# Two stage seams: order of ScalarE's last work, and which queue issues six sets of transfers

## The chip, the cores and the metric

The kernel runs on one core of one Trainium2 chip. The metric is the device time of one execution in microseconds; the median over runs is compared. The reference time of the kernel before is 3046.53 us, the median of 3 runs (3046.21 to 3046.75).

## The reference, cut to what matters

One transformer-like layer over 2048 latent tokens of width 1024, with 256 context tokens, in float32:

```python
h_x = (x * (1 + mx1) + mx0) @ w_in                    # input projection, 1824 columns
kv  = kv_side(h_x), same for the context               # rms norms, rotary, low-rank expansion by w_ukv
y   = mixer_out(h_x, kv, ...)                          # 6 + 6 attention heads, short conv, @ w_o
x   = layer_norm(ALPHA * x + mx2 * y) * ln1_g + ln1_b
y   = square(relu((x * (1 + mx4) + mx3) @ w_mlp1)) @ w_mlp2   # 1024 -> 4096 -> 1024
x   = layer_norm(ALPHA * x + mx5 * y) * ln2_g + ln2_b
```

Every large product is made of three products of rounded parts (high x high, high x low, low x high), so each operand is split into a "hi" tile (ScalarE copies it into the rounded type) and a "lo" tile (VectorE subtracts). The MLP's two products use seven block products of block sums in place of eight (a Strassen-like scheme): `NP = 7` positions, in the order `ORDER = (3, 5, 2, 4, 1, 7, 6)`.

## The kernel before, in words

The program is six stages, each one block of code with its own instruction stream for SyncE (SP), ScalarE (ACT), VectorE (DVE), GpSimd (POOL) and TensorE (PE): modulate, project, expand, attend, mix, mlp. A stage's block ends for all engines together; the next stage's instructions come behind it on every engine. The order of instructions inside an engine's stream is written out by hand, and semaphores join the streams. Nearly all transfers are issued by SP, a few by ACT; a transfer is issued when its engine's stream comes to it.

**Project (L260 to L608).** Eighteen token tiles of 128 (2 of context, 16 latent). PE projects a tile in four banks, ACT copies the banks out and squares, DVE and POOL normalise and rotate, PE turns the result, ACT rounds it (`out`, L395 on), DVE makes the low parts, SP stores both to DRAM. At the end (`last`) SP waits until everything on PE is done and the stores of tile 15 have landed, and then issues the first loads of the next stage: `load_ckv` part 0, `load_cq` 0, `load_ckv` part 1, `load_cs` 0, the keys of the first head, its queries (`gq_first`), `load_cq` 1, `load_cs` 1. `load_cs` brings the rotary tables of the expansion (384 KB each), `load_cq` the compressed queries of 512 tokens in two parts (512 KB each).

**Expand (L646 on).** Four blocks of 512 tokens. For each, PE makes the rotary part of the queries (it waits for `cq_in[b]`), three query tiles, three key tiles and six value tiles; DVE multiplies by the tables (waits for `cs_in[b]`). Between these, PE makes score products for the running maxima of the first head (L827), the first of which waits for the keys and `gq_first`. SP stores all results and loads what is next. Attend then begins with the loads of the first head (`load_heads`, issued by SP in block 2).

**Mix (L1680 on).** Sixteen token tiles s = 0 to 15. PE multiplies by w_o (L931), DVE adds the residual and normalises (L1906 to L1923), PE turns the normalised tile (L2000), ACT scales it into the MLP's input (`stream`, L1836, eight activations for a tile). Once a pair of tiles is there, POOL makes its block sums (L1967), ACT rounds each of the seven (`highs`, L1867), DVE makes the low parts (`lows`, L1944). Results go to a ring of three places in `area` and from there to DRAM (`s_uc`, SP, L1788), so `highs` waits until the store of three uses earlier has landed; the last sum of the last pair goes into a spare slot instead. ACT's last work of the stage, after the root of tile 15 (L1872), is in this order: `highs` of pair 6, positions 3 to 6; `stream(14)`; `stream(15)`. SP's last work is: stores of the sums at positions 3 to 6, then `load_slot` for positions 5 and 6, four transfers of 1 MB from DRAM into the slots that the MLP multiplies with.

**Mlp (L2016 on).** Its first product needs 32 turns (sixteen for each half); a turn is seven positions, each 12 matmuls of 512 columns (L2718). Positions 0 to 2 of turn 0 were already made in the mix stage (L1665). So PE begins with position 3: ACT rounds the weights (L2321), DVE makes their low part (L2474), PE multiplies. Position 5 waits for slot 5, position 6 for slot 6 (`slot_ready`). SP begins the stage with two semaphore increments for the weights (L2179) that were loaded in mix; POOL waits for them.

Of the kernel before, what the change touches and what calls it, by code (L numbers as in the profile page):

```python
# [210 lines left out]
def stage_project(nc, g, a):  # L211

    with ExitStack() as ctx:
# [56 lines left out]
        def schedule(eng, split, work, out, last, second_in=None):  # L270

            def step(i, c):
                n = i * 2 + c
                if c < CT + TT - 1 and (c != 1 or second_in is None):
                    split(n + 1, c + 1, i + (c + 1) // 2)
                if c == 0 and second_in == "step":
                    split(2, 2, 1)
                work(n, c, c >= CT)
                if c:
                    out(n - 1, c - 1, c > CT)  # L280
            for c in range(CT + 1):
                step(0, c)
            with eng.Fori(0, (TT - 2) // 2) as i:
                step(i, CT + 1)
                step(i, CT + 2)

            last(CT + TT - 1)
# [25 lines left out]
        @block.sync  # L313
        def _(sp):
            sp.dma_start(g_row[:, :], a["g_heads"]).then_inc(tables_in, 16)
            sp.dma_start(inv_n[:, :], a["inv_n"]).then_inc(tables_in, 16)
            sp.dma_start(cs[:, :, :], a["cs_tok"]).then_inc(tables_in, 16)
            for n in range(CT):
                sp.sem_inc(x_in[n], 16)

            def load(n, c):
                sp.wait_ge(ulo_set, n - 1)
                s = c % 2
                sp.dma_start(xt[s][:, :, :], a["x_t"][bass.ds(n - CT, 1)].rearrange("o p k t -> p (o k) t")).then_inc(x_in[s], 16)

            def store(n, is_x, highs=True):
                sp.wait_ge(hi_out, n + 1)
                sp.wait_ge(lo_out, n + 1)
                sp.wait_ge(v_set, n + 1)
                store_kv(sp, n)  # L330
                if is_x:
                    store_x(sp, n, parts=(0, 1) if highs else (1,), conv=highs)

            def step(i, c):
                n = i * 2 + c
                if c < CT + TT - 2:
                    load(n + 2, c)
                if c:
                    store(n - 1, c > CT, c < CT + TT - 1)
            for c in range(CT + 1):  # L340
                step(0, c)
            with sp.Fori(0, (TT - 4) // 2) as i:
                step(i, CT + 1)
                step(i, CT + 2)
            for c in range(CT + TT - 3, CT + TT):
                if c == CT + TT - 2:
                    sp.wait_ge(ulo_set, CT + TT - 1)
                    for done, (at, w, _, _) in zip(w_up_in, EXPANSION):
                        sp.dma_start(at, w).then_inc(done, 16)
                step(0, c)  # L350
            sp.wait_ge(bank_done, banks_before(CT + TT))
            sp.wait_ge(stored, stores_before(CT + TT - 2))
            load_ckv(sp, g, 0, slice(0, CTX))
            load_cq(sp, g, 0)
            load_ckv(sp, g, 1, slice(CTX, CTX + QB))
            load_cs(sp, g, a, 0)
            load_keys(sp, g, 0, g.first_heads_in, slice(0, EARLY_KEYS))
            for half, part in enumerate((slice(0, DH), slice(DH, P))):
                sp.dma_start(g.gq_first[part, :].bitcast(F32), g.qg[half][0:DH, 0:BLK]).then_inc(g.first_heads_in, 16)
            load_cq(sp, g, 1)  # L360
            load_cs(sp, g, a, 1)
            sp.wait_ge(hi_out, CT + TT)
            sp.wait_ge(lo_out, CT + TT)
            sp.wait_ge(v_set, CT + TT)
            sp.wait_ge(stored, stores_before(CT + TT - 1))

        @block.scalar
        def _(act):
            def split(n, c, pair):
                act.wait_ge(modulated, n + 1)  # L370
                need(act, bank_done, banks_before(n - 1))
                nc.scalar.activation(u_hi[c % 2][:, :, :], xt[c % 2][:, :, :], ACT.Copy).then_inc(uhi_set, 1)

            def copy_bank(n, c, b):
                act.wait_ge(bank_done, banks_before(n) + (b + 1))
                c0, cn = BANKS[b]
                nc.scalar.activation(h[c % 2][:, c0:c0 + cn], main[:, b, 0:cn], ACT.Copy).then_inc(bank_out, 1)

            def work(n, c, is_x, banks=len(BANKS)):
                at, hs = banks_before(n), h[c % 2]  # L380
                banks = banks if is_x else 1
                need(act, turned, n - 1)
                need(act, v_set, n - 1)
                for b in range(banks):
                    copy_bank(n, c, b)
                act.wait_ge(bank_out, at + banks)
                need(act, var_set, n)
                width = NORM if is_x else KVR + HKV * DH
                nc.scalar.activation(sq[:, 0:width], hs[:, O_CKV:O_CKV + width], ACT.Square).then_inc(squared, 1)
                if isinstance(n, int) and n == 0:  # L390
                    split(2, 2, 1)
                act.wait_ge(var_set, n + 1)
                nc.scalar.activation(rstd[:, :], var[:, :], ACT.Sqrt).then_inc(std_set, 1)

            def out(n, c, is_x):  # L395
                act.wait_ge(turned, n + 1)
                need(act, stored, stores_before(n))
                for q in range(3 if is_x else 1):
                    nc.scalar.activation(a_hi[:, q], tr_a[:, q * P:(q + 1) * P], ACT.Copy, scale=g.gcol[:, q:q + 1])
                nb = 4 if is_x else 1  # L400
                nc.scalar.activation(b_hi[:, 0:nb], tr_b[:, 0:nb * P].rearrange("p (c t) -> p c t", t=P), ACT.Copy)
                if is_x:
                    nc.scalar.activation(c_st[:, :], tr_c[:, :].rearrange("p (c t) -> p c t", t=P), ACT.Copy)
                nc.scalar.activation(k_hi[:, :], tr_k[0:ROPE, 0:P], ACT.Copy).then_inc(hi_out, 1)
                nc.scalar.activation(v_st[:, :], h[c % 2][:, O_GV:O_GV + P], ACT.Copy).then_inc(v_set, 1)

            def between():
                for done, (at, _, hi, _) in zip(w_up_in, EXPANSION):
                    act.wait_ge(done, 16)
                    nc.scalar.activation(hi, at, ACT.Copy).then_inc(w_up_hi, 1)  # L410

            def last(n):
                work(n, n, True, NORMED)
                out(n - 1, n - 1, True)
                act.wait_ge(hi_out, n)
                store_x(act, n - 1, parts=(0,))
                for b in range(NORMED, len(BANKS)):
                    copy_bank(n, n, b)
                between()
                out(n, n, True)  # L420
            schedule(act, split, work, out, last, second_in="work")
            act.wait_ge(lo_out, CT + TT)

# [209 lines left out]
def load_cq(eng, g, b):  # L633
    for half, t in enumerate((g.cq_hi, g.cq_lo)):
        eng.dma_start(t[b][:, :, :].bitcast(F32), g.cq[half][:, :, b * QB:(b + 1) * QB].rearrange("c p t -> p c t")).then_inc(g.cq_in[b], 16)


def load_cs(eng, g, a, b):
    eng.dma_start(g.e_cs[b][:, :, :], a["cs_rope"][:, :, b * QB:(b + 1) * QB]).then_inc(g.cs_in[b], 16)
# [980 lines left out]
NP = len(ORDER)  # L1620
SLOTS = 8
DIRECT = 3
# [54 lines left out]
def stage_mix(nc, g, a):  # L1677

    with ExitStack() as ctx:
# [81 lines left out]
        def first_half_stored(eng):  # L1761

            for e in range(RING):
                eng.wait_ge(uc_stored[e], 32 * ring_uses(ring_use(3, NP - 1) + 1, e))

        def load_slot(eng, j):

            for part, t in enumerate((g.slot_hi, g.slot_lo)):
                eng.dma_start(raw(t[slot_of(j)]), g.uc[0, j, part]).then_inc(g.slot_in[slot_of(j)], 16)

        @block.sync
        def _(sp):
            sp.dma_start(ln_cols[:, :], a["ln1_cols"]).then_inc(cols_in, 16)
# [33 lines left out]
            store_row(TT - 2)  # L1807
            store_sums(PAIRS - 1, range(0, BEHIND))
            store_row(TT - 1)
            store_sums(PAIRS - 1, range(BEHIND, NP))  # L1810
            first_half_stored(sp)
            sp.wait_ge(y_done, Y_ALL)
            for j in range(DIRECT + 2, NP):
                load_slot(sp, j)
            sp.wait_ge(cols_in, 16)
            sp.wait_ge(mlp_in, 32)

# [1 line left out]
        def _(act):  # L1819
# [48 lines left out]
            for s in range(TT):  # L1868
# [10 lines left out]
                if s == LEFT_AT:  # L1879
                    for pos in range(EARLY_LEFT):  # L1880
                        left_high(pos)
            highs(PAIRS - 1, range(BEHIND, NP))
            stream(TT - 2)
            stream(TT - 1)

        @block.vector
        def _(dve):
# [130 lines left out]
def stage_mlp(nc, g, a):  # L2018

    g.mix_sems.close()  # L2020
    with ExitStack() as ctx:
# [155 lines left out]
        def _(sp):  # L2177
            for q in range(2):
                sp.sem_inc(w1_in[q], 16)  # L2179

            def tail_stores():
                for pos in range(NP):
# [691 lines left out]
```

## Time and profile before

| | us |
|---|---|
| median of 3 runs | 3046.53 |
| the profiled execution | 3052.03 |
| its span | 3050.2 |
| PE busy | 2932.1 (96%) |
| DVE, ACT, POOL busy | 2270.0, 1327.7, 1380.3 |

The span is the time between the first and the last instruction of the profiled execution. A busy time is the sum of an engine's instructions. The seams between the stages are short: expand begins at 417 us, attend at about 495 us, mlp at 1793 us.

### The profile page before, as it was taken

The page shows a single profiled execution, that of the slowest core. Times are in us where ns is not written, and L with a number is a line of the kernel's source. Part 1 is how long each engine was busy: PE and PEld are TensorE (multiplying, and loading weights), DVE is VectorE, ACT ScalarE, POOL GpSimd, SP SyncE. Part 2 cuts the span into 40 slices and gives each one's busy share as a digit, 9 for nine tenths or more (in the row PEclk, how much of TensorE's full clock was granted, in tenths as well). Part 3 has the DMA queues.
Part 4 walks back from the last instruction along what each step waited for, and adds up shares of the span by engine and source line. Part 5 has one row for each costly group of instructions (what it writes and reads, how often), then busy time and mean ns, then how long its engine had stood idle before and what let it go on. Part 6 is the DMA issues. An engine that isn't in the chain of part 4 may idle for free. (4 is left out here: it accounts for less than half of the span.)

```text
span 3050.2 us, 43167 instructions
## 1 busy us (share of the span) xinstructions
PE 2932.1 (96%) x15760; PEld 2201.1 (72%) x15760; DVE 2270.0 (74%) x3170; ACT 1327.7 (44%) x1911; POOL 1380.3 (45%) x833
## 2 busy tenths in 40 slices
PE   5999978999999999999999989999999999999997
PEld 3889865566666566666658768887888888887886
DVE  4445456788887888788777788776777667887788
ACT  3222233444444444444443456555555543433452
POOL 1233324677767867686732244332333144214420
PEclk7999989999999999999999989999999999999998
DMA  6232379524354332434147885447444687897883
GB/s 262 60 87 78 101 234 325 120 74 81 98 119 95 78 81 63 85 80 85 30 149 254 285 311 205 155 152 292 152 153 153 221 299 287 288 315 278 301 289 131
DMA packets 252013, 526.65 MB, mean 173 GB/s; under 512 B 35568, under 2 KB 110832, under 8 KB 240624
## 3 DMA queue, kind: packets, MB, share of 16 engines
q1 hardware_dynamic: 243504, 493.55, 50.4%
q10 hardware_dynamic: 8320, 30.61, 2.6%
q8 instruction: 115, 1.88, 0.3%
q14 instruction: 74, 0.61, 0.1%
HBM read 363.19 MB, written 160.76 MB: 172 GB/s over the span
## 5 line engine op out<-in xcount | busy, mean ns | idle before, releaser
L1369 DVE TENSOR_REDUCE h_mpart<-a_mx 128x1 f32<-128x512 f32 x920 | 537.7, 632 | 153.4 <-PE a_mx L1474 140.6
L1298 POOL TENSOR_TENSOR a_acc_p<-a_acc_p,a_pf 128x1024 f32<-128x1024 f32 x237 | 572.6, 2416 | 152.1 <-ACT a_pf L1349 121.5
L1349 ACT ACTIVATE a_pf<-o_y 128x1024 f32<-128x1024 f32 x432 | 441.8, 1026 | 380.0 <-PE o_y L1521 372.6
L2662 POOL TENSOR_TENSOR stream<-raw_rows 128x512 f32<-128x512 f32 x158 | 217.3, 1377 | 374.6 <-DVE f_wx L2474 360.7
L2671 POOL TENSOR_TENSOR f_y<-f_y,raw_rows 128x1024 f32<-128x1024 f32 x72 | 196.5, 2730 | 350.1 <-DMA raw_rows<-in_w 350.1
L2726 PE MATMUL o_y<-slots 128*128 128x512 f32 x1176 | 298.1, 391 | 1.8 <-DVE slots L2481 1.8
L2718 PE MATMUL o_y<-slots,f_wx 128*128 128x512 f32 x1140 | 266.5, 392 | 4.8 <-DMA slots<-s_uc 4.8
L2726 PEld LDWEIGHTS o_y<-slots 128*128 128x128 f32 x1176 | 221.6, 189 | 49.4 <-DVE slots L2481 3.1
L2718 PEld LDWEIGHTS o_y<-slots,f_wx 128*128 128x128 f32 x1140 | 215.7, 189 | 50.3 <-DMA slots<-s_uc 5.2
L573 PE MATMUL p_main<-win_hi,u_hi 128*128 128x512 f32 (+2 forms) x528 | 196.8, 373 | 15.2 <-PEq L75 14.4
L573 PE MATMUL p_main<-win_hi,u_lo 128*128 128x512 f32 (+2 forms) x528 | 195.2, 370 | 0.0
L573 PE MATMUL p_main<-win_lo,u_hi 128*128 128x512 f32 (+2 forms) x528 | 195.1, 370 | 0.0
L2481 DVE TENSOR_TENSOR slots<-f_y,slots 128x1024 fp32r<-128x1024 f32 x98 | 140.9, 1438 | 71.6 <-ACT slots L2342 70.9
L1539 PE MATMUL a_o<-a_pf,h_gv 128*64 128x512 f32 x864 | 192.8, 595 | 0.0
L1539 PE MATMUL a_o<-a_pf,a_v 128*64 128x512 f32 x864 | 192.7, 595 | 0.0
L2342 ACT ACTIVATE slots<-f_y 128x1024 fp32r<-128x1024 f32 x98 | 104.0, 1061 | 196.6 <-POOL f_y L2671 189.3
L2479 DVE TENSOR_TENSOR slots<-raw_rows,slots 128x1024 fp32r<-128x1024 f32 x98 | 153.3, 1564 | 36.8 <-ACT slots L2334 36.1
L931 PE MATMUL o_y<-slots,low 128*128 128x512 f32 x768 | 179.8, 393 | 0.7 <-PEq L942 0.7
L931 PEld LDWEIGHTS o_y<-slots,low 128*128 128x128 f32 x768 | 143.7, 189 | 32.1 <-issue 2.7
L1521 PE MATMUL o_y<-h_gq,h_gk_hh 64*128 64x512 f32 x864 | 162.2, 402 | 0.2 <-ACT a_pf L1349 0.2
L2474 DVE TENSOR_TENSOR f_wx<-stream,f_wx 128x512 fp32r<-128x512 f32 x158 | 157.9, 999 | 0.6 <-ACT f_wx L2321 0.2
L2726 PE MATMUL o_early<-slots 128*128 128x512 f32 x588 | 151.7, 394 | 4.3 <-DVE slots L2481 4.3
(343 smaller groups left out, 6136.6 us busy)
## 6 DMA issues: line engine op xcount, KB each, us to landing
s_hx<-o_area SPq DMA_DIRECT2D x224, 256.0 KB, 2.6
raw_rows<-s_hx SPq DMA_DIRECT2D x112, 512.0 KB, 4.4
f_y<-in_w SPq DMA_DIRECT2D x104, 512.0 KB, 5.8
raw_rows<-in_w SPq DMA_DIRECT2D x72, 512.0 KB, 5.9
raw_rows<-in_w SPq DMA_DIRECT2D x32, 1024.0 KB, 4.9
s_uc<-o_area SPq DMA_DIRECT2D x76, 256.0 KB, 5.6
raw_rows<-in_w_ada SPq DMA_DIRECT2D x8, 2048.0 KB, 8.8
low<-s_mix SPq DMA_DIRECT2D x32, 512.0 KB, 5.2
```

What stands on the lines that cost most here:

```text
L573: mm = nc.tensor.matmul(main[:, b, 0:cn], lhs[s][:, k], rhs[:, k, c0:c0 + cn], start=(k == 0 and rhs is w_hi and lhs is u_hi), stop=(k == ...
L931: mm = nc.tensor.matmul(y[:, half, :], x_[s % 2][:, k], w_[k][:, half * 512:(half + 1) * 512], start=(k == 0 and n == 0), stop=(k == KD - ...
L1298: nc.gpsimd.tensor_tensor(acc[:, :], left[:, :], pf[(b * KT + kt) % NPF][:, :], ALU.add).then_inc(added_p, 1)
L1349: nc.scalar.activation(pf[n % NPF][:, :], sc[n % 2][:, :], ACT.Exp, scale=SCALES[0 if is_mla(b) else 1]).then_inc(exped, 1)
L1369: nc.vector.reduce_max(mpart[b % 2][:, s + 4 * half, k:k + 1], bank(("pair", c), half)[:, 0:CHUNKS[k][1]], AX.X).then_inc(mx_read, 1)
L1521: mm = nc.tensor.matmul(sc[n % 2][:, half * QB:(half + 1) * QB], w, y[strip, :], start=(m == 0), stop=(m == len(ops) - 1))
L1539: mm = nc.tensor.matmul(o_ps[half * DH:(half + 1) * DH, :], v[0 if is_mla(b) else 1][:, kt], pf[n % NPF][:, half * QB:(half + 1) * QB], st ...
L2474: nc.vector.tensor_tensor(lo, src, hi, ALU.subtract).then_inc(lo_set, 1)
L2662: nc.gpsimd.tensor_tensor(out, w1_part(n, first), w1_part(n, second), plus(sign)).then_inc(sum_set, 1)
L2671: nc.gpsimd.tensor_tensor(y1[cc % YN], y1[cc % YN], y2[k % Y2N], plus(sign)).then_inc(y_sum, 1)
L2718: mm = nc.tensor.matmul(by_pair(bank_at(m)), w[:, k], x[s][:, :, k * P:(k + 1) * P], start=(k == 0 and j == 0), stop=(k == 3 and j == 2))
L2726: mm = nc.tensor.matmul(bank_at(4 * (pr % 2) + tt), x[s][:, f, tok], y[s][:, 2 + f, :], start=(start and j == 0), stop=(stop and j == 2))
```

## The change

Three moves. (1) In mix, `stream(14)` comes on ACT ahead of the rounding at position 3 of the last pair, and `stream(15)` between the roundings at positions 3 and 4. (2) The store of the last sum (position 6) and the loads of slots 5 and 6 leave SP's stream in mix and come in mlp, behind its two semaphore increments; the waits that stood ahead of these loads in mix go too. (3) At the end of project, `load_cs` 0, `load_cq` 1 and `load_cs` 1 leave SP's stream and are issued by ACT, behind its last `out`.

```diff
@@ stage_project, sync
             load_cq(sp, g, 0)
             load_ckv(sp, g, 1, slice(CTX, CTX + QB))
-            load_cs(sp, g, a, 0)
             load_keys(sp, g, 0, g.first_heads_in, slice(0, EARLY_KEYS))
             for half, part in enumerate((slice(0, DH), slice(DH, P))):
                 sp.dma_start(g.gq_first[part, :].bitcast(F32), g.qg[half][0:DH, 0:BLK]).then_inc(g.first_heads_in, 16)
-            load_cq(sp, g, 1)
-            load_cs(sp, g, a, 1)
@@ stage_project, scalar, last
                 out(n, n, True)
+                act.wait_ge(bank_done, banks_before(n + 1))
+                load_cs(act, g, a, 0)
+                load_cq(act, g, 1)
+                load_cs(act, g, a, 1)
@@ stage_mix
+        def store_last_sum(eng):
+
+            p, pos = LAST_SUM
+            for part, at in enumerate(target(p, pos)):
+                eng.dma_start(by_tile(g.uc[p // 4, pos, part][:, p % 4, :]), raw(at)).then_inc(uc_stored[ring_use(p, pos) % RING], 16)
+        g.store_last_sum = store_last_sum
@@ stage_mix, sync
             store_row(TT - 1)
-            store_sums(PAIRS - 1, range(BEHIND, NP))
-            first_half_stored(sp)
-            sp.wait_ge(y_done, Y_ALL)
-            for j in range(DIRECT + 2, NP):
-                load_slot(sp, j)
+            store_sums(PAIRS - 1, range(BEHIND, NP - 1))
@@ stage_mix, scalar
-            highs(PAIRS - 1, range(BEHIND, NP))
             stream(TT - 2)
+            highs(PAIRS - 1, range(BEHIND, BEHIND + 1))
             stream(TT - 1)
+            highs(PAIRS - 1, range(BEHIND + 1, NP))
@@ stage_mlp, sync
             for q in range(2):
                 sp.sem_inc(w1_in[q], 16)
+            g.store_last_sum(sp)
+            for j in range(DIRECT + 2, NP):
+                uc_load(sp, j)
```

## Rows read from the trace of the kernel before

**Rows 1.** The page: busy time by engine; the span in 40 slices.
```profile
PE 2932.1 (96%) x15760; PEld 2201.1 (72%) x15760; DVE 2270.0 (74%) x3170; ACT 1327.7 (44%) x1911; POOL 1380.3 (45%) x833
PE   5999978999999999999999989999999999999997
```
**Rows 2.** Timeline at mlp's seam: start, us, engine line op [idle before <-releaser].
```profile
1787.23 0.68 DVE L1944 TENSOR_TENSOR slots<-o_rows,slots 128x512 fp32r<-128x512 f32 x1
1779.61 1.90 PE L2000 MATMUL o_y<-ident,o_area 128*128 128x128 f32 x8 [3.22 <-DVE o_area L1918]
1772.61 1.03 PE L2000 MATMUL o_t_x<-ident,o_area 128*128 128x128 f32 x8
1787.44 0.39 PE L1665 MATMUL o_y<-slots,o_left_lo 128*128 128x512 f32 x1
1794.91 5.45 PE L2718 MATMUL o_y<-low,f_wx 128*128 128x512 f32 x12 [7.08 <-DVE f_wx L2474]
1800.17 5.67 PE L2718 MATMUL o_y<-slots,f_wx 128*128 128x512 f32 x24
```
**Rows 3.** Chain of waits at the seam into mlp: start us, us, what.
```profile
1792.86 0.02 SPq L2179
1792.90 0.64 ACT f_wx L2321
1793.63 1.14 DVE f_wx L2474
1794.91 10.93 PE o_y L2718 x36
```
**Rows 4.** Timeline of ACT, end of mix.
```profile
1775.96 0.20 ACT L1872 ACTIVATE o_rstd<-o_var 128x1 f32<-128x1 f32 x1 [8.62 <-DVE o_var L1913]
1779.59 0.63 ACT L1867 ACTIVATE o_area<-o_area 128x512 fp32r<-128x512 f32 x1 [3.43 <-DMA s_uc<-o_area]
1784.81 0.64 ACT L1867 ACTIVATE o_area<-o_area 128x512 fp32r<-128x512 f32 x1 [4.58 <-DMA s_uc<-o_area]
1786.42 0.61 ACT L1867 ACTIVATE slots<-o_rows 128x512 fp32r<-128x512 f32 x1
1786.94 2.88 ACT L1836 ACTIVATE o_area<-o_t_x,o_u_cols 128x128 f32<-128x128 f32 x8
1789.68 2.93 ACT L1836 ACTIVATE o_area<-o_y,o_u_cols 128x128 f32<-128x128 f32 x8
```
**Rows 5.** Timeline of SP at the same seam.
```profile
1782.70 5.45 SPq L1788 DMA_DIRECT2D s_uc<-o_area  x6
1788.19 1.15 SPq L1788 DMA_DIRECT2D s_uc<-slots  x2
1789.52 2.26 SPq L1769 DMA_DIRECT2D slots<-s_uc  x4
```
**Rows 6.** Timeline of SP, end of project.
```profile
411.24 0.72 SPq L639 DMA_DIRECT2D e_cs<-in_cs_rope  x1
...
414.66 0.59 SPq L635 DMA_DIRECT2D e_cq_hi<-s_cq  x1
415.29 0.47 SPq L635 DMA_DIRECT2D e_cq_lo<-s_cq  x1
415.80 0.62 SPq L639 DMA_DIRECT2D e_cs<-in_cs_rope  x1
```
**Rows 7.** Timelines of PE and ACT around the start of expand.
```profile
417.12 0.55 PE L810 MATMUL e_ring<-e_ckv_hi,low 128*128 128x256 f32 x1 [9.51 <-PEq L213]
411.81 0.29 ACT L405 ACTIVATE v_st<-h 128x128 f32<-128x128 f32 x1
426.76 0.50 PE L827 MATMUL e_mx<-h_gk_hh,e_gq_first 128*128 128x512 f32 x1 [2.32 <-DMA e_gq_first<-s_qg]
```
**Rows 8.** Transfer issues at 1789.52 to 1791.78: count, KB, us to landing; first and last.
```profile
slots<-s_uc SPq DMA_DIRECT2D x1, 1024.0 KB, 6.5
slots<-s_uc SPq DMA_DIRECT2D x1, 1024.0 KB, 12.1
```
**Rows 9.** Stretches: us, busy by engine (PE PEld DVE ACT POOL), PEclk, DMA share, GB/s.
```profile
1780.00:1785.00 5.00, 5.00 (x21) 4.26 (x20) 2.64 (x3) 0.42 (x2) 0.00 (x0) 0.69 1.02 413
1794.90:1800.20 5.30, 5.29 (x13) 4.14 (x14) 4.55 (x3) 3.22 (x7) 5.30 (x4) 0.50 0.99 417
```
**Rows 10.** The same view of stretches, expand.
```profile
412.00:440.00 28.00, 18.46 (x66) 14.86 (x67) 13.39 (x25) 6.43 (x13) 4.89 (x3) 0.74 1.03 299
440.00:470.00 30.00, 28.43 (x120) 22.25 (x119) 21.38 (x35) 11.68 (x21) 7.45 (x5) 0.97 1.04 371
470.00:500.00 30.00, 21.49 (x88) 16.70 (x88) 16.99 (x31) 10.49 (x19) 10.45 (x11) 0.88 1.02 329
```
**Rows 11.** Transfers: `gq_first` (last, issued 414.0), `load_cs` 1 (415.80), `gk_ll` (487.81).
```profile
e_gq_first<-s_qg SPq DMA_DIRECT2D x1, 256.0 KB, 12.7
e_cs<-in_cs_rope SPq DMA_DIRECT2D x1, 384.0 KB, 15.5
h_gk_ll<-s_kg SPq DMA_DIRECT2D x1, 576.0 KB, 11.5
```
**Rows 12.** Timeline of PE, start of attend.
```profile
499.37 0.80 PE L1474 MATMUL a_mx<-h_gk_hh,h_gq 64*128 64x512 f32 x2 [0.81 <-DMA h_gk_ll<-s_kg]
```
**Rows 13.** Transfers in mix: ACT's load issued at 1772.8, SP's store at 1772.5.
```profile
low<-s_uc ACTq DMA_DIRECT2D x1, 1024.0 KB, 8.7
s_uc<-o_area SPq DMA_DIRECT2D x1, 256.0 KB, 10.7
```

## The prediction

> **What bounds the kernel now.** I began with the page [rows 1]. PE is busy for 2932.1 of 3050.2 us, and only the first slices and a few later ones are not full. Gaps on PE are therefore the only place where moved work on ACT or SP can pay, and all of them together are 118 us. The change touches two seams, so I next read the chain of waits and the timelines there.
>
> Into mlp: PE makes its last early product at 1787.44 + 0.39 = 1787.83 and its first mlp product at 1794.91, 7.08 us idle [rows 2]. The chain reads back from there: PE waits for DVE's low part, that for ACT's rounding at 1792.90, and this for SP's first instruction of the stage at 1792.86 [rows 3]. The reader is to see which engine was last in mix: ACT, whose second `stream` ends at 1789.68 + 2.93 = 1792.61 [rows 4]. DVE was done at 1787.91 [rows 2], SP at 1789.52 + 2.26 = 1791.78 [rows 5]. So it takes 0.3 us from the last engine's end to the next stage's start (1792.61 to 1792.90), and 2.0 us more until PE works (1792.90 to 1794.91).
>
> Into expand: SP is last. Its final issue ends at 415.80 + 0.62 = 416.42 [rows 6], and PE begins at 417.12 after 9.51 us idle; ACT was done at 412.10 [rows 7]. That is 0.7 us from SP's end to PE's work.
>
> **The change part by part.**
>
> *Streams on ACT.* ACT is idle for 3.43 us until 1779.59 and again for 4.58 us until 1784.81, both times because a store of the ring has not landed [rows 4]. `stream(14)` takes 2.88 us. What it reads has been there since before the root at 1775.96, so it runs from 1776.2 to 1779.1 and position 3 stays at 1779.59. `stream(15)` waits for PE's turning, which ends at 1779.61 + 1.90 = 1781.5 [rows 2]. It takes 2.93 us and ends at 1784.5, 0.3 us ahead of the ring's landing at 1784.81. Positions 4 to 6 stay where they are, the last at 1786.42 + 0.61 = 1787.03. Cost 0, covered by the two waits; without that cover it would be their 5.8 us, as before. ACT's end moves from 1792.61 to 1787.03, 5.6 us earlier.
>
> *Store and slot loads on SP.* SP's last issue in mix is now the store at position 5, which ends at 1782.70 + 5.45 = 1788.15 [rows 5]. DVE (1787.91) and PE (1787.83) end just ahead, so SP is last. The next stage starts at 1788.15 + 0.3 = 1788.45, and PE can begin at 1788.45 + 2.0 = 1790.45, which is 4.45 us earlier than 1794.91.
>
> What is late next: the slots. In mlp SP issues the two stores (1.15 us) and then the four loads (2.26 us), six transfers in all [rows 5]. The first load is issued at about 1788.5 + 1.15 + 0.15 = 1789.8, against 1789.52 before. From first issue to last landing it took before: last issued at 1791.3, landed 12.1 us later, at 1803.4; the first landed at 1789.52 + 6.5 = 1796.0 [rows 8]. The data thus comes no earlier than before: 1803.4 to 1803.7. Before, PE took up slot 6 after the 24 matmuls of positions 4 and 5, at 1800.17 + 5.51 = 1805.7, 2.3 us after the landing. Now position 3 runs from 1790.45 for 5.26 us (it took 1794.91 to 1800.17 [rows 2], at a granted clock of 0.50, the lower level of 1.2 GHz [rows 9]), positions 4 and 5 take 5.5 us, and PE stands ready for slot 6 at 1801.2. It waits 2.4 us, to 1803.6. The gain of the seam is 1805.7 - 1803.6 = 2.1 us, not 4.45. Half of it again may go: PE has a new pause of 2.4 us, and after the pause of 3.22 us at 1779.6 eight small matmuls took 1.90 us, as against 1.03 us for their like at 1772.61 [rows 2], and the granted clock of that stretch is 0.69, part of it at the lower level [rows 9]. I price the lower clock at 0.8 us, between 0 (the pause is short enough) and 1.6 us. Seam: -1.3 us, bounds -4.45 (slots come early) and -0.3.
>
> Behind ACT's first four roundings stands its wait for the last sum's store. This is now issued at 1788.5 rather than 1788.19 and ACT arrives 4.4 us earlier. The stores took some 4 us to land, to 1793.3, and ACT's fourth rounding ends at 1798.2 - 4.4 = 1793.8; cost 0. POOL's first sums only wait for the semaphore increments, which stand ahead of SP's transfers. SP's next weight load and tail stores come behind six issues rather than none, 3.4 us, but they begin 4.4 us sooner; cost 0.
>
> *Tables and queries on ACT's queue.* SP drops four issues: 0.72 + 0.62 us [rows 6] for the tables and about 1.1 us for the two of `load_cq`, with gaps 2.6 us. It ends at 413.9. ACT gets four issues behind 412.10, at 0.5 to 0.6 us each: it ends at 414.4. Expand starts at 415.1 instead of 417.1. This is 2.0 us on PE, and I count none of it as a gain. The stretches show why [rows 10]: the DMA share is 1.03, 1.04 and 1.02 in the three stretches from 412 to 500 us. Every transfer waits in a backlog, 15.5 us for the last table [rows 11]. Attend begins on a transfer too: `gk_ll`, issued at 487.81, lands 11.5 us later at 499.3, and PE's first product of attend starts at 499.37 [rows 11, 12]. The change moves no byte away and starts none before 412, when the DMA engines are already full. What ends the stage is the total of bytes by the rate. So: 0 us. Bounds: below, 2.0 us gained, if attend follows PE; above, 3 us lost, as in the second rival.
>
> The Trainium skill bears on this ("DMA: Bandwidth & Descriptors", section "Queues, rings and completion order"): each DMA engine serves its queues in turn, a packet at a time, so a second queue adds no bandwidth but lets its transfers overtake those of the first. By that rule the loads on ACT's queue would share the engines with `gq_first`, which two of the three stood behind; the sum would then be that of the second rival. This trace has it in mix only, and agrees there: the store below took 10.7 us.
>
> **Sum.** -1.3 + 0 = -1.3 us. Against the profiled execution's 3052.03 us (a span of 3050.2 and 1.8 around it) this is 3050.7; its distance to the median of the runs, 5.5 us, is that of profiling and the same on both sides. From the median: 3046.53 - 1.3 = 3045.2 us. Behind both seams PE's slices are at nine tenths or more [rows 1], so I take it that what is won at a seam stays.
>
> **The rivals.**
>
> *Both seams pay in full.* Landing is set by the time of issue and not by the backlog, and DMA in expand catches up. For it: the first pause of 7.08 us is real and ACT alone ends it. Against it: landings at 1803.4 and 499.3, each within 2.4 us of the need. -4.45 - 2.0 = -6.4 us, 3040.1 us. Chance 0.10. One seam in full and the other as forecast, -3.3 to -4.5 us, 3042 to 3043 us: 0.20.
>
> *The other side: the first score product waits for `gq_first`.* Place: PE at 426.76, where it already waits 2.32 us for this very transfer [rows 7]. Of the bytes on ACT's queue, 384 KB stood ahead of it before; the other 1.4 MB (1024 + 384 KB) stood behind, and landed 4.6 us later (426.7 to 415.80 + 15.5 = 431.3) [rows 11]. If both queues share the engines evenly, `gq_first` lands near 431, up to 4.6 us late, and PE with it. Of this PE can win back what it waited for other things in this block, about 1.9 us; the rest, 2.7 us, counts from the point at which SP's stores come so late that the DMA backlog runs dry. Then +2.7 - 1.3 = +1.4 us, 3047.9 us; with a further pause of PE's clock, up to 3049. For it: in mix a store of 256 KB on SP's queue took 10.7 us to land while ACT's queue had its loads of 1 MB under way [rows 13], against 4 us at the end of the stage, so the two queues do share. Against it: the backlog later in the stage (11.5 us for `gk_ll` [rows 11]) is far longer than 2.7 us. Chance 0.18.
>
> *Nothing comes of it.* The pause for slot 6 costs the whole gain in clock (1.6 us) and landing is 0.3 us later: 0 to -0.3 us, 3046.4 us. Chance 0.15.
>
> The forecast, -0.5 to -2.5 us, has the remaining 0.37.
>
> **How the numbers follow.** The range takes in one seam paid in full together with most of the other (-6) and the second rival with its clock term (+2.5): 3040.5 to 3049.0. Outside is part of the first rival and what no row shows. 0.2% is 6.1 us, about what a measurement of this kernel can tell from no change. Faster by more needs both seams in full: of the 0.10 a little over half, 0.06. Slower by more would need a loss that no row bounds: 0.03. Within 0.2%: 0.91.
>
> **What the changed profile would show.** ACT's last activation of mix near 1787.0, the `stream` groups at 1776.2 and 1781.6 (all times shifted by whatever project brings), and SP as the last engine. PE's gap into mlp falls from 7.1 to about 2.6 us, and a new wait of 2 to 3 us appears before position 6, put down to `slots<-s_uc`. If that wait is missing, I was wrong on the landing and the gain is 4 us. In expand PE starts 2 us earlier, its wait at the first L827 is longer than 2.32 us, and the first product of attend stands within 1 us of 499.4. If it stands at 497.4, DMA was not the bound; if it stands beyond 501, the second rival holds.

## The result: slower by about 7 us, and the profile after

| | before | after |
|---|---|---|
| median of 13 runs each, side by side | 3044.9 | 3052.7 |
| lowest to highest | 3041.1 to 3050.5 | 3045.8 to 3057.6 |
| span of the profiled execution | 3050.2 | 3053.1 |

The ratio is 1.0024, with an interval of 1.0015 to 1.0033: 7.3 us slower, between 4.6 and 10. The forecast was 1.3 us faster. Single runs of one kernel lie up to 10 us apart or more, so the spans of single profiles do not rank kernels here. What a profile can give is the distance between two events of one seam, and I read it that way throughout.

The page of the changed kernel says what [rows 1] said: the same work, and PE busy nearly all the time.

```profile
PE 2932.0 (96%) x15760; PEld 2202.2 (72%) x15760; DVE 2264.5 (74%) x3170; ACT 1328.5 (44%) x1911; POOL 1378.3 (45%) x833
PE   5999978999999999999999979999999999999997
```

**The seam into expand.** First the timeline of SP: its first and last loads at the end of project, then the stores of the late tile and the next loads of expand.

```profile
409.57 0.49 SPq L631 DMA_DIRECT2D e_ckv_hi<-s_ckv  x1
414.21 1.30 SPq L358 DMA_DIRECT2D e_gq_first<-s_qg  x2
...
419.54 2.88 SPq L699 DMA_DIRECT2D s_kn<-e_st_hi  x1
422.46 4.87 SPq L699 DMA_DIRECT2D s_kn<-e_st_lo  x1
437.56 0.35 SPq L631 DMA_DIRECT2D e_ckv_hi<-s_ckv  x1
```

SP ends its project work at 415.5 now (it was 416.42 [rows 6], with the stage 1.3 us later as a whole). Between 427.3 and 437.56 it issues nothing. The view of waits says for what: a store of the queries' low part. Before the change it was the last of SP's own late stores (`s_vg<-v_st`, issued at 424.61, landed 8.6 us later) that let SP go on, at 433.23. Now that store has landed at 434.2 (419.02 + 15.2), and the wait goes on for another 3.3 us. The columns are us in total, times, longest.

```profile
SPq L631 <- DMA s_qg<-b_lo: 10.2, 1, 10.2
```

Who issued that store? ACT did. Its timeline shows the four new transfers, and then the four stores of tile 15 that ACT always had to make at the start of expand (`late_x`, L294 and L295; SP stores the rest).

```profile
411.46 0.70 ACTq L640 DMA_DIRECT2D e_cs<-in_cs_rope  x1
412.19 0.76 ACTq L636 DMA_DIRECT2D e_cq_hi<-s_cq  x1
412.98 0.88 ACTq L636 DMA_DIRECT2D e_cq_lo<-s_cq  x1
413.89 0.60 ACTq L640 DMA_DIRECT2D e_cs<-in_cs_rope  x1
...
418.51 0.45 ACTq L294 DMA_DIRECT2D s_cq<-a_hi  x1
419.00 0.49 ACTq L295 DMA_DIRECT2D s_qg<-b_hi  x1
419.52 5.48 ACTq L294 DMA_DIRECT2D s_cq<-a_lo  x1
425.03 2.32 ACTq L295 DMA_DIRECT2D s_qg<-b_lo  x1
427.39 0.60 ACT L738 ACTIVATE e_st_hi<-e_ring 128x512 fp32r<-128x512 f32 x1 [8.51 <-issue]
```

The reader is to see the second numbers. Issuing a store of 128 KB took 5.48 us and the next one 2.32 us, where the two before them took 0.45 and 0.49. ACT itself stands still for 8.51 us ("issue"). Before the change the same two issues took 0.51 and 0.49 us and the last of them began at 420.89. The view of transfers gives its landing: the last store took 12.5 us, so it landed at 425.03 + 12.5 = 437.5, which is when SP goes on.

```profile
s_qg<-b_lo ACTq DMA_DIRECT2D x1, 192.0 KB, 12.5
```

The stretches of the changed kernel show what this does to the DMA engines (columns as in [rows 9]; [rows 10] has 1.03 for the first).

```profile
412.00:440.00 28.00, 17.93 (x59) 14.28 (x60) 11.28 (x22) 7.50 (x16) 4.86 (x3) 0.71 0.94 257
434.00:436.00 2.00, 2.00 (x7) 1.56 (x7) 1.05 (x2) 0.20 (x1) 0.00 (x0) 0.69 0.99 328
436.00:438.00 2.00, 2.00 (x10) 1.60 (x10) 1.29 (x2) 1.89 (x4) 0.58 (x1) 1.00 0.10 34
438.00:440.00 2.00, 1.78 (x9) 1.31 (x8) 1.91 (x4) 1.63 (x4) 1.80 (x1) 1.00 0.69 169
```

From 436 to 438 us the engines have next to nothing to do (share 0.10, 34 GB/s). The same slices of the kernel before:

```profile
434.00:436.00 2.00, 1.35 (x7) 0.90 (x5) 0.19 (x1) 0.82 (x2) 1.86 (x1) 1.00 0.91 222
436.00:438.00 2.00, 0.75 (x4) 0.66 (x4) 2.00 (x4) 1.14 (x3) 0.00 (x0) 1.00 1.00 396
```

This profile is the mildest of the five with the old project end. In the others (e2, e3, e5 and g1, below) the thinnest slice of 2 us between 432 and 440 us has a share of 0.83, 0.51, 0.32 and 0.37. So the old order thins at this place too. What sets the change apart is how much is lost: from 412 to 440 us the five have shares of 0.98 to 1.03, and the three profiles with this move 0.94, 0.92 and 0.92.

On PE (to be laid beside [rows 7] and [rows 12]): expand begins earlier, the first score product later, and attend later.

```profile
416.21 0.55 PE L811 MATMUL e_ring<-e_ckv_hi,low 128*128 128x256 f32 x1 [6.42 <-PEq L213]
429.74 0.79 PE L828 MATMUL e_mx<-h_gk_hh,e_gq_first 128*128 128x512 f32 x1 [5.63 <-DMA e_gq_first<-s_qg]
...
503.23 0.79 PE L1475 MATMUL a_mx<-h_gk_hh,h_gq 64*128 64x512 f32 x2
```

I count from SP's first load of the seam, to be free of what came before it. PE starts 6.6 us behind it (8.9 before), `gq_first` is there at 20.2 (18.5), attend's first product at 93.7 (91.1). So the move does start PE 2.2 us sooner, and the stage ends 2.5 us later.

Attend's first product waits for no transfer in the changed kernel. The loss comes in earlier, where ACT has to wait for the landing of a store of queries before it rounds the next ones (first line before, second after):

```profile
483.38 1.08 ACT L737 ACTIVATE e_st_hi<-e_ring 128x512 fp32r<-128x512 f32 x2 [6.29 <-DMA s_qn<-e_st_lo]
486.88 1.08 ACT L738 ACTIVATE e_st_hi<-e_ring 128x512 fp32r<-128x512 f32 x2 [7.64 <-DMA s_qn<-e_st_lo]
```

Counted from SP's first load this is 75.1 us before and 77.3 after (77.6 in e1 and 77.3 in e4, which have the same move). Thirteen of the fourteen profiles have this wait, and in all of them attend's first product follows 15.7 to 17.1 us behind it. Most of the 2.5 us is thus there at a transfer's landing. I have not followed wait by wait how the dry slice at 436 us leads to the late landing at 486.

**The seam into mlp.** ACT (beside [rows 4]), SP (beside [rows 5]) and PE (beside [rows 2]), in three fences.

```profile
1779.25 2.89 ACT L1840 ACTIVATE o_area<-o_t_x,o_u_cols 128x128 f32<-128x128 f32 x8
1789.50 0.63 ACT L1871 ACTIVATE o_area<-o_area 128x512 fp32r<-128x512 f32 x1 [7.36 <-DMA s_uc<-o_area]
1790.03 2.89 ACT L1840 ACTIVATE o_area<-o_y,o_u_cols 128x128 f32<-128x128 f32 x8
1792.78 0.66 ACT L1871 ACTIVATE o_area<-o_area 128x512 fp32r<-128x512 f32 x1
...
1793.81 0.66 ACT L1871 ACTIVATE slots<-o_rows 128x512 fp32r<-128x512 f32 x1
```
```profile
1790.95 5.09 SPq L1796 DMA_DIRECT2D s_uc<-o_area  x6
1796.69 0.82 SPq L1776 DMA_DIRECT2D s_uc<-slots  x2
1797.56 2.21 SPq L2124 DMA_DIRECT2D slots<-s_uc  x4
```
```profile
1775.93 1.03 PE L2005 MATMUL o_t_x<-ident,o_area 128*128 128x128 f32 x8
1798.58 5.46 PE L2726 MATMUL o_y<-low,f_wx 128*128 128x512 f32 x12 [11.13 <-DVE f_wx L2482]
1803.84 6.06 PE L2726 MATMUL o_y<-slots,f_wx 128*128 128x512 f32 x24
1811.81 5.74 PE L2726 MATMUL o_t_x<-slots,f_wx 128*128 128x512 f32 x24 [1.91 <-DMA slots<-s_uc]
```

`stream(14)` lies in the first wait, as meant. Then the ring's place for position 3 is free 13.6 us after the turning of tile 14 (1789.50 - 1775.93), against 7.0 us before (1779.59 - 1772.61 [rows 2, 4]). When it comes, the places for the next positions are free too, so `stream(15)` stands in nobody's shadow: position 4 follows directly behind it. PE's pause into mlp is 11.13 us, where 7.08 was to become 2.6. SP is the last engine of the stage, and PE's wait for slot 6 is there, 1.91 us. From the turning of tile 14 to position 6 it is 35.9 us, against 33.1.

### The profile page after: what moved, and what is told of

Read it like the earlier page. It is cut to its first block and busy times, and to the rows that moved or that the text cites. A ratio compares the mean times of both kernels' runs of the same rounds, so it can differ in the third digit from the quotient of the medians.

```text
span 3053.1 us, 43165 instructions
## 1 busy us (share of the span) xinstructions
PE 2932.0 (96%) x15760; PEld 2202.2 (72%) x15760; DVE 2264.5 (74%) x3170; ACT 1328.5 (44%) x1911; POOL 1378.3 (45%) x833
## 5 line engine op out<-in xcount | busy, mean ns | idle before, releaser
L574 PE MATMUL p_main<-win_hi,u_hi 128*128 128x512 f32 (+2 forms) x528 | 197.7, 374 | 15.1 <-PEq L75 14.4
L2489 DVE TENSOR_TENSOR slots<-f_y,slots 128x1024 fp32r<-128x1024 f32 x98 | 148.7, 1518 | 69.8 <-ACT slots L2350 69.0
```

Source lines behind the costliest of these rows:

```text
L574: mm = nc.tensor.matmul(main[:, b, 0:cn], lhs[s][:, k], rhs[:, k, c0:c0 + cn], start=(k == 0 and rhs is w_hi and lhs is u_hi), stop=(k == ...
L2489: nc.vector.tensor_tensor(slot_lo[s][:, 2:4, :], y1[cc % YN], slot_hi[s][:, 2:4, :], ALU.subtract).then_inc(clo, 1)
```

## The experiments

Ratios are to the kernel before, run beside them on the same chip, with their intervals; 0.1% is 3 us. Two distances of each profile are read besides: **A**, from SP's first load of the seam to attend's first product (before 91.1; the five profiles with the old project end have 90.1 to 92.0), and **B**, from the turning of tile 14 to position 6 in mlp (before 33.1).

### The parts alone

*e1_project: only move 3.*

```diff
 # stage_project, sync
-            load_cs(sp, g, a, 0)
-            load_cq(sp, g, 1)
-            load_cs(sp, g, a, 1)
 # stage_project, scalar, last
                 out(n, n, True)
+                act.wait_ge(bank_done, banks_before(n + 1))
+                load_cs(act, g, a, 0)
+                load_cq(act, g, 1)
+                load_cs(act, g, a, 1)
```

> Only the third move: the tables and load_cq 1 on ACT's queue at the end of project, all else as before. From SP's first load of the seam (s_ckv to e_ckv, 408.24 us before, 409.57 after the whole change) to PE's first product of attend it took 91.1 us before and 93.7 us with the whole change. Theory (the queues share, gq_first comes late): 93 to 95 us here too, PE's wait at the first L827 near 5.6 us instead of 2.3 us, and the run 2 to 5 us slower than before. Rival (the loss is in mix): 91 to 92 us and a run within 1.5 us of before.

Measured: 1.0017 (1.0008 to 1.0027), 5.2 us slower. A is 94.0. ACT's issues stall as in the whole change, and the DMA engines run dry at the same point:

```profile
417.88 6.43 ACTq L294 DMA_DIRECT2D s_cq<-a_lo  x1
424.34 2.73 ACTq L295 DMA_DIRECT2D s_qg<-b_lo  x1
427.12 0.60 ACT L738 ACTIVATE e_st_hi<-e_ring 128x512 fp32r<-128x512 f32 x1 [9.82 <-issue]
```
```profile
434.00:436.00 2.00, 2.00 (x8) 1.45 (x7) 1.29 (x2) 0.43 (x2) 0.00 (x0) 0.81 0.28 92
436.00:438.00 2.00, 2.00 (x10) 1.60 (x10) 1.32 (x3) 2.00 (x4) 0.47 (x1) 1.00 0.31 41
```

This one move is slower by itself.

*e2_mix: moves 1 and 2, project as before.*

```diff
 # stage_mix, sync
-            store_sums(PAIRS - 1, range(BEHIND, NP))
-            first_half_stored(sp)
-            sp.wait_ge(y_done, Y_ALL)
-            for j in range(DIRECT + 2, NP):
-                load_slot(sp, j)
+            store_sums(PAIRS - 1, range(BEHIND, NP - 1))
 # stage_mix, scalar
-            highs(PAIRS - 1, range(BEHIND, NP))
             stream(TT - 2)
+            highs(PAIRS - 1, range(BEHIND, BEHIND + 1))
             stream(TT - 1)
+            highs(PAIRS - 1, range(BEHIND + 1, NP))
 # stage_mlp, sync, behind the two increments
+            g.store_last_sum(sp)
+            for j in range(DIRECT + 2, NP):
+                uc_load(sp, j)
```

> Only the first two moves: stream(14) and stream(15) between the roundings, last store and slot loads in mlp; project as before. In the profile of the whole change the ring store that ACT waits for at position 3 landed 15.3 us after its issue, against 8.9 before, and PE took up position 6 about 2.2 us later, counted from its last turning of tile 14. Theory (that landing was chance, the mix part gains): the landing is again near 9 us, position 6 comes 31 to 33 us after that turning (33.1 before, 35.9 with the change) and the run is 0 to 2 us faster than before. Rival (the mix part itself makes the stores late): landing near 15 us again and the run 2 to 4 us slower.

Measured: 1.0002 (0.9991 to 1.0014). A 91.1, B 35.0. `stream(15)` is in the open here too (1782.55 for 2.88, right behind position 3), and PE waits 1.96 us for slot 6. The ring's place for position 3 is free 12.5 us behind the turning of tile 14, so the late landing was not chance, and B lies above the 31 to 33 that I expected. The runs show no gain and no loss.

*e3_streams: move 1 alone* (the lines of stage_mix, scalar, above).

> Only the first move: the two streams between the roundings; SP's stores and slot loads stay in mix. Theory: ACT ends 5.6 us sooner, the stage then ends with SP's slot loads at 1791.8 (0.8 us sooner than ACT before), PE's pause into mlp is 6.3 us instead of 7.1, run -1 to 0 us. Rival (the new order on ACT delays the roundings and with them the ring's stores): run 1 to 4 us slower.

Measured: 0.9994 (0.9981 to 1.0006). B 34.5. ACT is done early, but the next stage can't begin: SP still has the last stores and the slot loads in mix, and ACT waits for it. In the profile the move costs about 1 us (the old order has a B of 33.4 in the mean, below): `stream(15)` is in the open and holds up positions 4 to 6, and SP's last work with them. That is the rival's mechanism, at a size that the runs do not show.

```profile
1798.68 0.63 ACT L2322 ACTIVATE f_wx<-raw_rows 128x512 fp32r<-128x512 f32 x1 [5.79 <-SPq L2180]
```

*e4_whole: the whole change once more*, beside the three above.

> The whole change once more, for a second profile beside the single moves on one chip. Theory: time slower than before by the project part alone (2 to 5 us) less what mix gains; the expand stretch is again 93 to 94 us; the late landing in mix (15.3 us) does not come back. Rival: it comes back and costs its 3 us in this profile too, and the run is 6 to 9 us slower than before.

Measured: 1.0017 (1.0006 to 1.0029). A 94.1, B 34.5, DMA share 0.92 from 412 to 440 us. Position 3 is free 12.7 us behind the turning of tile 14.

*e5_spmove: move 2 alone* (the lines of sync above, the streams last as before).

> Only the second move: last store and slot loads in mlp; the streams stay last in mix. The two moves together gave no difference (ratio 1.0002), the streams alone none (0.9994). Theory: ACT's streams end mix as before at 1792.6, the slot loads start behind it some 4 us later than before, PE waits for slot 6 by 3 to 4 us, run 2 to 4 us slower. Rival (the wait is taken up by later waits for DMA): within 1 us of before.

Measured: 1.0006 (0.9994 to 1.0019), no difference that the runs show. B is 37.2, the longest: ACT is last again with its streams, and the slot loads stand behind it. In the profiles a move on SP needs the one on ACT, and the other way round.

### What in move 3 costs

*f1_tables: only the two tables on ACT's queue*; `load_cq` 1 stays on SP, as its last load.

```diff
 # stage_project, sync
-            load_cs(sp, g, a, 0)
             load_cq(sp, g, 1)
-            load_cs(sp, g, a, 1)
 # stage_project, scalar, last
+                act.wait_ge(bank_done, banks_before(n + 1))
+                load_cs(act, g, a, 0)
+                load_cs(act, g, a, 1)
```

> As the project part alone, but only the two tables (768 KB) go to ACT's queue; load_cq 1 stays on SP, last as before. With all three loads on ACT's queue, ACT took 5.5 and 2.3 us to issue its two late low stores at 419.5, SP waited 9.0 to 10.2 us for the last of them and went on at 437 us instead of 433, and the DMA share fell to 0.1 to 0.3 in 434 to 438. Theory (ACT's late stores stand behind its loads and all next loads wait for them): less ahead of them, so SP goes on at 434 to 436, first product of attend 1 to 2 us later than before, run 0 to 3 us slower. Rival (late gq_first alone is the cost): gq_first still shares with the tables, and the run stays some 5 us slower.

Measured: 0.9999 (0.9984 to 1.0014). A 91.6. `gq_first` is late here too (the two halves took 14.4 us to land, 12.1 before, 14.3 after) and PE waits 4.94 us for it. But ACT's late stores are issued without a stall (0.53 and 0.49 us), SP goes on 25.4 us behind its first load, as before, and the DMA share from 412 to 440 is 1.01. A late `gq_first` by itself costs next to nothing. The stall is now on SP, whose queue has `load_cq` 1 again: its last four late stores took 1.40, 2.62, 1.67 and 1.71 us to issue.

*f2_later: nothing on ACT's queue*; `load_cq` 1 and `load_cs` 1 stay on SP and are issued in expand, behind SP's late stores and its first store of key parts.

```diff
 # stage_project, sync
-            load_cq(sp, g, 1)
-            load_cs(sp, g, a, 1)
 # stage_expand, sync, behind store_set(1, 3, g.kn, slice(0, CTX))
+            load_cq(sp, g, 1)
+            load_cs(sp, g, a, 1)
```

> Kernel before, with load_cq 1 and load_cs 1 on SP still, but in expand behind the late stores and the first key store, so ahead of SP's wait for the late stores. cs 0 stays where it was; nothing on ACT's queue. Theory: the stage seam is 1.7 us sooner, gq_first lands as before or sooner, the late stores have 1.4 MB less ahead of them and land 3 to 4 us sooner, SP goes on at 428 to 430, DMA never runs dry; the first row of attend comes 1 to 3 us sooner and the run is 1 to 3 us faster than before. Rival (DMA is full, order plays no part): within 1 us of before.

Measured: 0.999 (0.9979 to 1.0001), the lowest of all, not quite clear of no change. A 91.3; SP goes on at 429.42.

*f3_behind_stores: three of the four transfers stay on ACT's queue, but behind its late stores*; `load_cs` 0 as in the change.

```diff
 # stage_project, scalar, last
+                load_cs(act, g, a, 0)
 # stage_expand, scalar
             g.late_x(act)
+            load_cq(act, g, 1)
+            load_cs(act, g, a, 1)
```

> Table 0 on ACT's queue at the end of project as in the change; load_cq 1 and table 1 on ACT's queue too, but in expand, behind ACT's late stores. Theory: only the place behind the late stores matters: ACT issues them without a stall, SP's wait for them is 5 us as before or shorter, it goes on at 430 to 433, and the run is within 1.5 us of before or faster. Rival (sharing the engines with gq_first is the cost): the loads still share with it from 421 us on, so the first score product is 1 to 3 us late and the run 2 to 4 us slower.

Measured: 0.9997 (0.9983 to 1.0011). A 88.7. The stores go out first and land by 430.1; SP goes on at 430.17, 21.3 us behind its first load of the seam (408.90), where it was 25.0 before the change and 28.0 after. ACT is held up by its issues nearly as long (7.22 us), so that hold alone is not what costs.

```profile
418.87 0.51 ACTq L294 DMA_DIRECT2D s_cq<-a_lo  x1
419.41 0.49 ACTq L295 DMA_DIRECT2D s_qg<-b_lo  x1
419.94 2.43 ACTq L634 DMA_DIRECT2D e_cq_hi<-s_cq  x1
...
425.50 0.60 ACT L736 ACTIVATE e_st_hi<-e_ring 128x512 fp32r<-128x512 f32 x1 [7.22 <-issue]
```
```profile
412.00:440.00 28.00, 19.49 (x70) 15.36 (x71) 13.99 (x26) 7.59 (x16) 4.87 (x3) 0.78 1.04 316
```

### Can the seams pay?

*g1_both_first: moves 1 and 2, but both streams ahead of position 3*, since the ring is late.

```diff
             stream(TT - 2)
-            highs(PAIRS - 1, range(BEHIND, BEHIND + 1))
             stream(TT - 1)
-            highs(PAIRS - 1, range(BEHIND + 1, NP))
+            highs(PAIRS - 1, range(BEHIND, NP))
```

> The mix and mlp moves, but both streams stand ahead of the rounding at position 3; project as before. From PE's last turning of tile 14 to position 6 of the first mlp turn it took 33.0 to 34.2 us in five profiles with the old order, 34.5, 35.0 and 35.9 in the three with both moves. In all but the profile of before the ring's landing came 9.5 to 13.6 us after that turning, not 7.0, and stream(15) then stands in the way for 2.9 us. Theory (the landing is late and the stream between positions 3 and 4 is paid in full): 2 to 3 us less than with both moves, so 32 to 33 us, run 0 to 2 us faster than before. Rival (the slot loads alone decide): 34.5 to 36 us still.

Measured: 1.0008 (0.9995 to 1.0021). B 33.0: both streams lie in the wait now, and B is still what it was before the change. The slots set it (PE waits 1.95 us for slot 6).

*g2_combined: g1's mix with f3's project.*

> The previous kernel's mix with table 0 on ACT's queue in project and load_cq 1 and table 1 on ACT's queue in expand, behind ACT's late stores (the project form that took 88.7 us from SP's first load to attend's first product, against 90.1 to 92.0 in five profiles with project as before and 93.7 to 94.1 with the change). Theory: both add up, 2 to 5 us faster than before. Rival (later waits for DMA take it up): within 1.5 us of before.

Measured: 0.9998 (0.9985 to 1.0011). A 87.8, the shortest of all, B 33.0; the time is that of before.

*g3_early_slots: g2, with the loads of slots 5 and 6 issued in mix, ahead of the stores of positions 3 to 5.*

```diff
 # stage_mix, sync
             store_row(TT - 1)
-            store_sums(PAIRS - 1, range(BEHIND, NP))
             first_half_stored(sp)
             ...
                 load_slot(sp, j)
+            store_sums(PAIRS - 1, range(BEHIND, NP - 1))
```

> As g2, but SP issues the loads of slots 5 and 6 in mix, behind the last row store and ahead of the stores at positions 3 to 5; only the last store is in mlp. Theory (position 6 waits for loads issued after the stage's end): no wait for slots, position 6 comes 29 to 32 us after the turning of tile 14. Rival (4 MB of loads ahead of the last ring stores): the stores land up to 10 us later, ACT's wait for them in mlp grows and PE waits for evacuated banks; run no faster than g2 or slower.

Measured: 1.0019 (1.0008 to 1.003), slower by 5.8 us. A is 92.0 with the same project and expand code that gave 88.7 and 87.8, so the 3 us that those two seemed to win do not repeat. The slots are there in time and B is 30.5. But the stores now stand behind 4 MB of loads: the last sum's store took 11.6 us where it took 3.8, ACT waits for it, and PE stops in the middle of position 6.

```profile
1809.44 0.60 ACT L2367 ACTIVATE stream<-o_early 128x512 f32<-128x512 f32 x1 [8.27 <-DMA s_uc<-slots]
```
```profile
1813.82 4.61 PE L2727 MATMUL o_t_x<-slots,f_wx 128*128 128x512 f32 x12 [3.43 <-DVE f_wx L2483]
```

*g4_later_both: g1's mix with f2's project.*

> The mix of g1 with f2's project form: nothing on ACT's queue, load_cq 1 and table 1 on SP behind the late stores. f2 alone had ratio 0.9990 (0.9979 to 1.0001). Theory: 2 to 5 us faster than before, as g2. Rival (nothing adds up): within 1.5 us of before.

Measured: 0.9999 (0.9988 to 1.001). A 91.0, B 32.0. No version of the twelve is clearly faster than the kernel before. In the five with loads behind the late stores (f2, f3, g2, g3, g4) SP goes on at 21.3 to 22.3 us instead of 25 and the DMA share from 412 to 440 is 1.04 or 1.05. Even so, A is anything from 87.8 to 92.0. Fuller queues at this one place are not a gain that can be relied on.

## Why the prediction was wrong, step by step

**Tables and queries on ACT's queue: the step that failed.** I put it at 0, with +3 as the bound. Its parts held: PE starts 2.2 us earlier (2.0 forecast), `gq_first` is late, and the wait at the first score product grew from 2.32 to 5.63 us. I then set the second rival aside because "the backlog later in the stage (11.5 us for `gk_ll` [rows 11]) is far longer than 2.7 us". That is the backlog at 487 us. The one that counts is that of 433 to 438, where SP's next loads stand behind a wait for the stores of the late tile, so that the queue holds only what was issued earlier; with the old order it already thins there (a share of 0.91 in the profile before, down to 0.32 in e5). And I had left out the path of those stores that ACT issues, on the very queue on which 1.8 MB were newly put ahead of them. For SP I had asked what is queued behind each move; for ACT's queue I had not. The last of them lands at 437.5 instead of 431.9 (420.89 + 11.0), SP resumes 3.0 us later counted from its first load (28.0 against 25.0), and the DMA engines stand idle for some 2 us. That is the second rival's ending (+2.7 against 2.5, 2.9 and 3.0 us measured as A in three profiles), reached by another queue than the one it named.

f3 bears this out: the same bytes on the same queue, three of the four transfers behind the stores, and neither the dry slice nor the loss is there. In f3 `gq_first` is also no longer late (12.2 us), but f1 shows that a late `gq_first` is not enough. In the timed runs the interval of f2 lies wholly below that of e1. Those of f1 and f3 overlap it at its lower end (1.0008 against 1.0014 and 1.0011). If the half widths are combined as for independent errors, an estimate, f3 lies 0.0020 (within 0.0017) below e1 and f1 0.0018 (within 0.0018). So f3 is just clear of e1 and f1 is on the edge, and the profiles carry the rest of the reading.

The Trainium skill says in "DMA: Bandwidth & Descriptors" (section "Queues, rings and completion order") that each DMA engine takes its queues in turn, packet by packet. The trace agrees: with ACT's queue filled, the same `gq_first` took 14.3, 15.0 and 15.7 us to land, not 12.1. The same page of the Trainium skill says in its section "Rules for kernel authors" that spreading transfers over issuing engines saves issue time only. Here it saved 2.2 us of it, and cost more, since ACT's stores stood behind the loads in its queue.

**Streams on ACT.** `stream(14)` cost nothing, as forecast. `stream(15)` was to end 0.3 us ahead of the ring's landing at 1784.81; it costs 2.9 us in the open. The mis-sized term is the landing for position 3: 7.0 us behind the turning of tile 14 in the one profile that I had, 9.5 to 13.7 us in twelve others, of either order (in the thirteenth, g4, ACT comes to it at 11.3 and the place is free). The second wait, 4.58 us before position 4, was as unusual: where no stream stands between, ACT waits 0 to 2.2 us for the next place in the others. With streams and roundings both on ACT the order between them then matters: as changed, B is 35.9, 34.5 and 35.0; in the old order 33.1, 34.2, 33.8, 33.1 and 33.0; with both streams first (g1, g2, g4) 33.0, 33.0 and 32.0.

**Store and slot loads on SP.** SP became the last engine, and PE's wait for `slots<-s_uc` before position 6 is 1.91 us (2.4 forecast, and 1.96 and 1.58 in the other two). The gain was to be 2.1 us. With both streams hidden (g1) it is 0.1, or 0.5 against the old order's mean: the slots land no sooner, because SP reaches their loads behind stores that wait for the ring. The clock term was mis-sized too. I priced the new pause before position 6 at 0.8 us. Behind it the granted clock is 1.00 (1811.8 to 1817.4 us), and the 24 matmuls took 5.74 us against 5.60 before: 0.1 us. The stretch behind the pause into mlp is at 0.50 after as before.

**The sum.** In the profiles move 3 costs 2.8 us (mean of 2.5, 2.9 and 3.0) and the mix moves 1.7 us (35.1 less the old order's 33.4), together 4.5. The runs give 7.3 (4.6 to 10) and, the second time, 5.2 (1.8 to 8.8). e1 alone gave 5.2 (2.4 to 8.2), which holds the 2.8. So 4.5 lies inside the second interval and just below the first. Whether some 2 us more are lost behind the seams stays open: the stretch from attend's first product to tile 14 varies between 1270.3 and 1277.0 us from profile to profile, the one from position 6 to the end by up to 19, and nothing of 2 us can be found in them. The range ended at 3049.0; it took the second rival's price as its end and did not add the exposed stream or what a profile can't resolve. The 5.5 us between the profiled execution and the median, which I put down to profiling, are no constant: e2's profiled execution took 3036.97 us, the lowest of its twelve.

## What to carry to other kernels

Before transfers are moved to another engine's queue, list what that engine itself has to issue next and who waits for it; stores that gate somebody's next loads must stay ahead of loads that nobody needs soon. A stage bound by transfers loses time where the queues run empty, so look for the wait in the issuing stream at which the backlog is thinnest, not at the longest backlog of the stage. A thin slice is a place to look, not yet a cost: e5 has a share of 0.32 from 432 to 434 us and the lowest A of its order, 90.1. A wait for a store's landing that is to cover other work should be read in several profiles; here it was 7 us in one and 9.5 to 13.7 in twelve others.

## What the hardware showed that I had not expected

- Issuing a transfer can hold the engine. With four loads (1.8 MB) just put on ACT's queue, its stores of 128 and 192 KB took 5.48 and 2.32 us to issue (6.43 and 2.73 in e1, 6.38 and 2.39 in e4), not 0.5, and ACT did no other work for 8.5 to 9.8 us. With the two tables alone ahead (768 KB, f1) it did not happen on ACT, but on SP, whose queue then had the other 1 MB. Before the change, too, SP's stores of 16 KB at 418.00 and 421.78 us took 2.27 and 2.78 us to issue. While ACT was held at 419.52, SP's stores of 384 KB took 2.88 and 4.87 us, so the rows do not tell a queue that is full from two engines that issue at once.
- Stores are held up by loads on either queue: 256 KB took 3.8 us to land at the start of mlp, 11.6 us behind 4 MB of loads on SP's own queue (g3), and 10.7 us in mix beside loads on ACT's queue [rows 13].
- One distance in a profile varies with nothing changed in front of it: A 88.7, 87.8 and 92.0 for the same project and expand code (f3, g2, g3). A difference of 3 us in one profile needs a second.
